# Another order of the half products in the second projection of a one-core diffusion and mixture-of-experts kernel

## The reference, cut to what matters

```python
def swiglu(h, w_gate_up, w_down):
    gu = h @ w_gate_up
    g, u = jnp.split(gu, 2, axis=-1)
    return (jax.nn.silu(g) * u) @ w_down      # w_down: 2816 x 1024
...
h = h + g_f * swiglu(...)                     # 256 latent tokens
hc = hc + cg_f * swiglu(...)                  # 256 context tokens
```

## Time and profile before

| | |
|---|---|
| median of 3 runs | 2140.92 us (2139.96 to 2141.46) |
| the profiled execution | 2140.95 us, span 2138.8 us |
| TensorE matmul busy | 1934.0 us, 90% of the span |
| TensorE weight load busy | 1388.0 us |
| VectorE busy | 816.2 us |
| ScalarE busy | 296.1 us |
| stage `down0` on TensorE | 671.91 to 784.00 us of the span |

### The profile page before, as it was taken

The page is one execution under the profiler, slowest core; times in us unless marked ns, Lnnn a source line. Parts: engine busy times, 40 slices in busy tenths (PEclk is TensorE's granted clock), DMA queues, the critical chain, the costliest instruction groups (busy, mean ns, idle before and its releaser), DMA issues.

```text
span 2138.8 us, 23354 instructions
## 1 busy us (share of the span) xinstructions
PE 1934.0 (90%) x9268; PEld 1388.0 (65%) x9268; DVE 816.2 (38%) x1504; ACT 296.1 (14%) x710; POOL 68.5 (3%) x122
## 2 busy tenths in 40 slices
PE   8999999999999999998999999999999886676665
PEld 5586465788888785684888888886887532222221
DVE  6697796668678224128212102126113200000001
ACT  2200281200100001007100000014001100000000
POOL 1011000000000011000000000000000000000000
PEclk9999999999999999999999999999999788877886
DMA  9455303344353144320344534441464799999996
GB/s 351 167 208 176 118 1 128 103 158 173 141 190 122 54 145 108 128 89 21 109 155 149 182 123 139 156 139 59 148 264 191 304 401 422 422 422 422 422 422 275
DMA packets 86019, 422.72 MB, mean 198 GB/s; under 512 B 9840, under 2 KB 9968, under 8 KB 60912
## 3 DMA queue, kind: packets, MB, share of 16 engines
q1 hardware_dynamic: 70416, 364.10, 44.8%
q0 software_dynamic: 15520, 57.45, 7.7%
HBM read 420.47 MB, written 2.95 MB: 198 GB/s over the span
## 4 chain that ended last, share of the span: by engine, by line
PE 73%; DMA 17%; DVE 7%; issue 2%; ACT 1%; SPq 1%; DVEq 0%; ACTq 0%
PE ps L701 28%; DMA ring<-in_up 9%; PE ps L723 7%; PE ps L937 6%; PE ps L836 5%; DMA ring<-in_down 4%; DMA ring<-in_gate 4%; PE ps L1297 3%; PE ps L745 3%; PE ps L755 3%; PE ps L785 3%; PE ps L776 2%; PE ps L1030 2%; PE ps L1048 2%; PE ps L1072 2%
## 5 line engine op out<-in xcount | busy, mean ns | idle before, releaser
L701 PE MATMUL ps<-xn,ring 128*128 128x256 f32 (+1 forms) x1376 | 308.2, 385 | 3.0 <-ACT xn L1409 1.7
L701 PEld LDWEIGHTS ps<-xn,ring 128*128 128x128 f32 x1376 | 260.5, 190 | 49.0 <-issue 10.4
L701 PE MATMUL ps<-big,ring 128*128 128x256 f32 x736 | 163.2, 384 | 11.7 <-DMA ring<-in_memkv 10.2
L701 PEld LDWEIGHTS ps<-big,ring 128*128 128x128 f32 x736 | 141.4, 193 | 32.4 <-DMA ring<-in_memkv 10.2
L701 PE MATMUL ps<-aux,ring 128*128 128x257 f32 x704 | 153.4, 380 | 0.0
L1297 PE MATMUL ps<-ring,aux 128*32 128x512 f32 x624 | 95.2, 740 | 56.4 <-DMA ring<-in_up 47.5
L701 PEld LDWEIGHTS ps<-aux,ring 128*128 128x128 f32 x704 | 133.6, 190 | 19.1 <-issue 0.4
L2304 DVE TENSOR_TENSOR work<-work,ps 128x512 f32<-128x512 f32 x8 | 8.4, 1044 | 351.4 <-PE ps L1297 351.4
L937 PE MATMUL ps<-ring,xn 128*128 128x512 f32 x256 | 113.9, 601 | 5.5 <-ACT xn L1413 4.0
L1790 DVE SCALAR_TENSOR_TENSOR aux<-aux,scond 128x1024 f32<-128x1024 f32 x84 | 103.0, 1276 | 5.3 <-DMA aux<-in_ada 5.2
L1297 PEld LDWEIGHTS ps<-ring,aux 128*32 128x32 f32 x624 | 21.5, 122 | 126.7 <-issue 126.7
(11 more groups left out here) (345 smaller groups left out, 2786.4 us busy)
## 6 DMA issues: line engine op xcount, KB each, us to landing
ring<-in_gu SPq DMA_DIRECT2D x88, 512.0 KB, 3.3
ring<-in_up SPq DMA_DIRECT2D x44, 1024.0 KB, 25.3
aux<-in_ada POOLq DMA_DIRECT2D x80, 512.0 KB, 4.9
ring<-in_gate SPq DMA_DIRECT2D x34, 1024.0 KB, 24.0
ring<-in_wqkv SPq DMA_DIRECT2D x48, 512.0 KB, 4.9
ring<-in_down SPq DMA_DIRECT2D x32, 704.0 KB, 4.2
ring<-in_win SPq DMA_DIRECT2D x44, 512.0 KB, 3.2
xn<-in_gate SPq DMA_DIRECT2D x14, 1024.0 KB, 19.0
```

Of the source, the lines that this page charges most:

```text
L701: mm = pe.matmul(ps[:, bank(s, c), 0:T], ring[:, slot(s.u0, j), k * P:(k + 1) * P], rhs(kk), start=kk == 0, stop=kk == nk - 1)
```

## The change

On TensorE the order becomes: first 0, first 1, rows, second 0, turn, fourth 0, others 0 with second 1 put between its S1*T1 and its S4*tokens product, fourth 1, first 2, others 1, fourth 2, second 2, others 2. On ScalarE the copy of `first(1)` moves ahead of the copy of the modulation rows. Nothing is added or taken away.

```diff
                     product(ps[:, b + 2, LAT:TOK], sums("S1"), sums("T1"), first=False, last=False).then_inc(s_pq, 1)
+                    if m == 0:
+                        second(1)
                     pe.wait_ge(s_up, order(s, m) + 1)
                     product(ps[:, b + 2, LAT:TOK], sums("S4"), tokens_of(1, late), first=False).then_inc(s_used, 4)
 
                 tsums = 2 * list(token_sums).index(s.name)
-                for m in range(2):
-                    first(m)
-                    second(m)
-                    between(m)
+                first(0)
+                first(1)
+                between(0)
+                second(0)
+                between(1)
                 for m in range(3):
-                    if m == 2:
-                        first(m)
                     if m == 0:
                         pe.wait_ge(s_tsum, tsums + 1)
                     fourth(m)
-                    if m == 2:
-                        second(m)
                     if m == 0:
                         pe.wait_ge(s_tsum, tsums + 2)
+                    elif m == 1:
+                        first(2)
+                    else:
+                        second(2)
                     others(m)
...
             first_half(st["down0"], 0)
+            first_half(st["down0"], 1)
             mod_rows(5)
-            first_half(st["down0"], 1)
             act.wait_ge(s_part, NORM["n2c"]["n"])
```

## The result

The changed kernel takes 2131.11 us (median of 6 runs, 2130.51 to 2136.09) against 2140.44 for the kernel before (6 runs); the ratio is 0.9965 with a 95% interval of 0.9952 to 0.9978, which is a gain of 4.7 to 10.3 us. The profiled execution of the changed kernel took 2135.11 us, span 2132.7, which is 6.1 less span than before.

The account below looks back on a forecast made before the run. TensorE, busy 90% of the span, was taken as the bound, with gaps in this stage. Winnable 7.73 us less new stalls of 1.47 and 1.40 gave a 4.86 gain, 2140.95 to 2136.1 us; range 2134.2 to 2138.6.

Parts of the forecast that it names:

- Head: Stage start, first 0 to fourth 0: waits on ScalarE's copies, 0.91 and 0.80 us, vanish.
- First new stall: S2*T2 of pair 0 waits 1.47 us for VectorE's weight sums, which second 1 covered before.
- Pair 0: Five products from S2*T2 to fourth 1 at 4.75 us each; the 1.12 lost on line 1975 is won.
- Pair 1: After fourth 1, first 2 waits 1.40 us for its weights (unit 8), landing 5.7 us after issue.
- rival 1: Unit 8, first 2's weights, lands in 4.0 us; no second stall, gain 6.26, time 2134.7; chance 0.13.
- rival 3: Unit 8, first 2's weights, lands after 8.3 us; stall 4.0 plus clock loss 1.58, gain 0.7, 2140.3; chance 0.07.
- Pair 1, weight sums, and pair 2: S2*T2 of pair 1 no longer waits on weight sums; fourth 2 and second 2 cover pair 2's with 1.43 to spare.
- the 3.32: Time in us lost before S2*T2 of pair 1, waiting on the weight sums; forecast to go.
- The clock: Low clock behind pair 1's weight-sum stall, 1.58 us, goes; the new stalls of 1.47 and 1.40 cost no clock.
- rival 2: Clock loss of 1.58 stays, returns at some stall, or wasn't typical before; gain 3.3, 2137.7; chance 0.22.
- From the stage to the whole time: Later stages all shift together, so the whole 4.86 us arrives: 2140.95 to 2136.1.
- half a microsecond of scatter: Scatter assumed around the total's forecast gain of 4.86 us, leaving about a quarter of its chance within no change.

Follow-up runs that it names:

- sums_first: Changed kernel with VectorE's weight sums of pair 0 moved ahead of T3, and TensorE's wait for T3 moved after S2*T2; 2127.51 us, ratio 0.9950.
- only_first2: Kernel before with only first 2 moved between fourth 1 and others 1, second 2 between fourth 2 and others 2; 2131.85 us, ratio 0.9966.
- only_head: Kernel before with only the head reordered (first 0, first 1, rows, second 0, second 1, turn) and ScalarE's copies exchanged; 2136.79 us, ratio 0.9983.
- only_second1: Kernel before with only second 1 moved between S1*T1 and S4 of pair 0; 2138.02 us, ratio 0.9988.
- before_again: Kernel before, unchanged, timed against itself; 2138.74 us, ratio 1.0004.
- split_second2: Changed kernel with pair 0's weight sums ahead of T3 and 3 of second 2's 11 steps ahead of pair 1's S4; 2128.34 us, ratio 0.9951.
- first2_early: Changed kernel with first 2 ahead of fourth 1; 2138.16 us, ratio 1.0000.
- before_shift: Kernel before with 46 already satisfied waits at the head of TensorE's stream; 2139.35 us, ratio 0.9994.
- the six shifts of the changed order: Changed kernel with 2, 6, 12, 24, 36 or 46 already satisfied waits heading TensorE's stream; stages 105.77 to 105.79 us; with 46, 2133.11 us.

## Why the prediction was right and wrong, point by point

*Head.* Right. The two waits on ScalarE's copies are gone: first 1 starts 4.75 after first 0, and second 0 follows the rows by 1.86.

*First new stall.* Right: 1.47 forecast, and 695.22 - 689.14 - 4.64 = 1.44 found, 0.11 after line 1956 (1953 before) ends. sums_first shows its cause, the token sum T3 ahead of the weight sums.

*Pair 0.* Right: (718.85 - 695.22) / 5 = 4.73 for each of the five products, with no wait on line 1978.

*Pair 1: the step that failed.* I wrote that unit 8 "landed 5.7 us later" and took this as the price: a stall of 1.40. It landed after 4.2, fourth 1 covers 4.35, and the stall measured nothing. This is rival 1, given 0.13; its gain of 6.26 is the stage's 6.32. The mechanism was right, the term was mis-sized. I chose the row of the very same issue over the one at 672.32 and did not ask what was peculiar to it. The trace before held the answer three times: its page gives a median landing of 4.2 for all 32 units of `in_down`, four units were issued together again at 750.04 and landed their first after 4.1, and one instruction packet of 1.45 us stood at 720.4. In rival 3, too, I gave unit 8 a price that isn't a first unit's: the four issued from 720.27 landed after 5.7, 8.3, 8.3 and 9.5.

The fit of the Trainium skill ("DMA: Bandwidth & Descriptors", section "Anatomy of one DMA — SWDGE (gpsimd) path"), an estimate of 3.65 us, lies 0.5 to 0.6 below the 4.1 to 4.3 of an undisturbed unit 8 here. Its consequence, no stall, was the right one.

*Pair 1, weight sums, and pair 2.* Right: the 3.32 is gone (only_first2: 4.92 less, with the clock's 1.58), the weight sums of pair 2 are covered by fourth 2 and second 2.

*The clock.* Right for the changed kernel: the granted clock is 1.00 from 672.30 to 778.07, the stall of 1.4 us included. Too simple for the kernel before: the fall behind its 3.35 us stall, worth 1.58, came in three profiles of the order before, and not in only_head and only_second1. The part of rival 2 that doubted it was right in kind, though it didn't decide: at the stall of 2.74 us the same kernel kept the clock in one execution (1.00) and not in another (0.70, before_again).

*From the stage to the whole time: the second step that failed.* The stage's gain arrived in the pair of profiles (6.3 in the stage, 6.1 in the span). But with the landing put right the sum gives rival 1's 2134.7, which lies inside the range; the measured 2131.11 lies another 3.6 below. What put the time out of the range is the last term. I took three runs, 1.5 us apart, as the base and for "half a microsecond of scatter", and the kernel's executions spread over 12 us. A median of six is uncertain by about 1 us or more on this account alone, an estimate from that spread. The base was high: 82 runs of the kernel before have a mean of 2139.6, not 2140.95, which accounts for 1.3 of the 3.6. The other groups of the changed kernel (2130.42, 2132.86) lie 1.8 to 4.3 below 2134.7 too. What makes up the rest, scatter or something behind the stage that the order speeds up, stays open.

## What to carry to other kernels

Lay the new order out product by product with the trace's own durations: it gave every wait of the stage but one to 0.1 us, and the stages of only_first2, sums_first and split_second2 to 0.05. It missed where the clock behind a stall was not what the first profile showed (only_head, only_second1, first2_early). Where a term rests on one transfer's landing, look at all the landings of that kind, the page's median first, and at what else the DMA engines carried at that moment, before taking it as a price. And when runs of a kernel scatter over several microseconds, read what a stage gains from that stage in the profile, don't take it for the gain of the whole, and give a range for the total that is as wide as the scatter of its medians.

## What the runs showed of the hardware that was not expected

A block of instructions loads as one packet of 16 KB and keeps one of the 16 DMA engines busy for 0.9 to 1.45 us. Where it began 0.15 to 0.51 us after the issue of a 704 KB unit, that unit landed 1.4 to 1.9 us late in three of four profiles (5.7, 6.0, 5.8 against 4.1 to 4.3) and about 0.2 late in the fourth (4.4). A block that began 0.18 to 2.34 us before the issue did nothing to that unit (seven profiles, before_shift and the six shifts of the changed order), but where it began 0.18 to 0.42 before, the unit issued next landed after 6.4 to 7.7, against 5.4 to 5.6 with the block 1.1 us or more ahead.

The same stall of 3.35 us cost the clock in three profiles and not in two, and the same stall of 2.74 us in one execution of the kernel before and not in another. The Trainium skill ("TensorE: Matmul & The Clock Gate", section "Part 1: The HAM clock gate") says that the monitor isn't aligned with the kernel; the two executions at the stall of 2.74 us agree with it (1.00 and 0.70). The cost of a fall depended on the case too: 1.58 us (before) and 1.35 (before_again, 5.64 for loads that take 4.29) behind 3.35 us of stall, 2.31 behind 4.58.
